# The second pair of layers of a four-layer network: from whole stages over 256 tokens to two blocks of 128 tokens, an MLP of one beside a mixer of the other

## The chip, the cores and the metric

The kernel is one program on 1 core of one Trainium2 chip, all in fp32. The metric is device time in microseconds (us). A core has five engines that run their own instruction streams in order and meet by semaphores: PE (TensorE, matrix products), ACT (ScalarE), DVE (VectorE), POOL (GpSimd) and SP (SyncE, which here only issues transfers). PEld is TensorE's loading of weights, which can overlap a matmul.

## The reference

Two networks of two layers follow each other. The first (a chunk MLP, a gated linear attention and two mixtures of experts) isn't touched. The second takes x of 256 tokens by 1024 and does:

```python
h = mixer_sb_ssm(x, ...)                     # mixer one
x = layer_norm(ALPHA * x + h)
x = layer_norm(ALPHA * x + square(relu(x @ w1[0])) @ w2[0])     # MLP one, 1024 -> 4096 -> 1024
h = mixer_dsa(x, ...)                        # mixer two
x = layer_norm(ALPHA * x + h)
x = layer_norm(ALPHA * x + square(relu(x @ w1[1])) @ w2[1])     # MLP two

def mixer_sb_ssm(x, w_in, ..., w_out):
    q, k, v, u = split(x @ w_in, 4)          # 512 wide each
    a = stick_breaking_attention(q, k, v)    # 8 heads; keys strictly before the query
    y = gelu(s5_ssm(u))                      # complex linear recurrence along the tokens, 16 x 128 states
    y = y * sigmoid(y @ w_glu + b_glu)
    return concat(a, y) @ w_out

def stick_breaking_attention(q, k, v):       # per head
    z = q @ k.T * scale
    log_1mb = where(s < t, log_sigmoid(-z), 0)
    log_w = log_sigmoid(z) + (sum of log_1mb over the later s)
    return where(s < t, exp(log_w), 0) @ v

def mixer_dsa(x, w_in, w_out):               # keys up to and with the query
    q, k, v, qi, ki, wi = split(x @ w_in)
    score = sum over 8 index heads of relu(qi @ ki.T) * wi
    keep the 64 keys of highest score; 16 heads of softmax attention with a slope on distance
    return o @ w_out
```

A token needs only tokens before it, so everything of tokens 0 to 127 can be done before anything of tokens 128 to 255. The state of the recurrence and the keys and values are all that the second block takes from the first.

## The kernel before

`write` replays one schedule for each engine; a method of the schedule is a no-op on engines that have no part in it. Generators yield at the end of a beat, and `run` and `together` advance several works by one beat in turn, so a beat sets the order in which an engine's instructions stand. There is no planner: this order is the order of each queue. Buffers are rings (`Slots`): a user waits until the last user of its slot is done. `W` is the ring of weights, five slots of 1 MB, filled by SP's queue.

The second pair of layers is `sb_ssm`, `mlp(0)`, `dsa`, `mlp(1)`, called one after another, each over all 256 tokens. Each begins with `barrier`, at which every engine, SP too, waits for all others; so the first weights of a stage are asked for behind it. Then the 16 transposes of x (`flip`, L993).

In `sb_ssm` the u columns (L1006), the coefficients and 16 `drive` steps come first; then `state_space` and `attention` run by beats. The recurrence is cut into 16 chunks of 16 tokens: 15 local steps (DVE operations of 256 elements, 8 to a step, L2026), 15 carries of 16 elements, 15 spread steps of 240 elements. The attention does two groups of four heads: scores (L1183), logarithms (ACT), `sb_beta` (POOL's `affine_select`, L2251, sets what lies above the diagonal to zero), running sums by a triangular matrix on PE (L1192 to L1194) added on DVE (L2087), exponent (ACT, L1569), `sb_weights` (the same select), and the products with v (L1203). The select takes 128 x 2048 numbers. Then the state's read-out (L1245), the gate, the output product (L1216 and L1231, each holds half of its 1024 rows) and the norm (L1686 to L1700).

In `mlp` the up half (L1006) has 256 matmuls with 256 moving columns, each 128 x 128 weights; ACT takes the relu (L1597), DVE the square (L2127). The down half (L1260) has 128 matmuls with 512 moving columns, then the add (L2136) and the norm.

In `dsa` the index columns (L1296, L1304), eight index heads (L1316, tiles of 32 rows) beside the q, k and v columns (L1006), the choice of 64 keys on DVE (L2172), and then 16 heads: products (L1325), four transposes (L1335), products with v (L1346), with DVE at L2182 to L2198; then the output product (L1231) and the norm.

## Time and profile before

| | |
|---|---|
| median of 3 runs | 3744.42 us (3741.61 to 3750.64) |
| the profiled execution | 3742.3 us, its span 3741.1 us |
| granted TensorE clock, mean | 0.836 |
| PE, PEld busy | 2684.1 us (72%), 1155.0 us (31%) |
| DVE, ACT, POOL busy | 2001.4 us (53%), 709.8 (19%), 1495.8 (40%) |
| moved by DMA | 1043.47 MB, mean 279 GB/s, up to 409 GB/s in one of 40 slices |
| second pair of layers | from 2827.2 us to the end |

The shares are over the whole span, three quarters of which are the first network; for a question about the second they have to be read from stretches. The chain of waits goes back from the last instruction to what released it, so each piece in it was on the path; idle time elsewhere costs nothing. Two instructions of PE stand for each fp32 matmul in the counts (x504 are 252 matmuls).

### The profile page before, as it was taken

Reading aid. Unit: us, or ns where it says so; the run is one execution under the profiler, and the core shown is the slowest. Engines: PE = TensorE matmul, PEld = TensorE weight load, DVE = VectorE, ACT = ScalarE, POOL = GpSimd, SP = SyncE. Lnnn points to the kernel's source line nnn. Section 1 sums busy time; section 2 is a strip of 40 time slices with the busy share of each in tenths; the row PEclk is TensorE's granted clock in tenths of the full one; section 3 lists DMA queues with packets and bytes.
Section 4 is the critical chain, followed back from the end, with each engine's and each line's share of the span. In section 5 each row is a group of like instructions: output and inputs, shape, how many; then the busy total and the mean of one; then the engine's idle time right before and its main releaser. Section 6 shows DMA issues by size and latency. Waiting matters only on the chain. (4 is left out here: it accounts for less than half of the span.)

```text
span 3741.1 us, 31922 instructions
## 1 busy us (share of the span) xinstructions
PE 2684.1 (72%) x11240; PEld 1155.0 (31%) x11240; DVE 2001.4 (53%) x4678; ACT 709.8 (19%) x1726; POOL 1495.8 (40%) x1563
## 2 busy tenths in 40 slices
PE   7758787787556776665687575565658369988898
PEld 2213332221112321111343221111116238555673
DVE  1155576654767677876214577777655941017201
ACT  0012222311113322211221121121113211004100
POOL 0034465554776676677200267767760010000000
PEclk9869988799877897767798687777678689999999
DMA  8577898999999999999432599999993104431343
GB/s 289 195 266 281 336 353 331 343 390 397 409 409 348 382 409 370 353 409 409 187 135 79 192 357 409 409 374 398 409 409 132 45 34 169 164 123 68 108 162 113
DMA packets 330484, 1043.47 MB, mean 279 GB/s; under 512 B 31748, under 2 KB 33028, under 8 KB 329812
## 3 DMA queue, kind: packets, MB, share of 16 engines
q0 software_dynamic: 221184, 805.40, 55.6%
q1 hardware_dynamic: 108724, 235.79, 17.5%
q8 instruction: 90, 1.47, 0.2%
q14 instruction: 70, 0.57, 0.0%
q10 hardware_dynamic: 416, 0.23, 0.0%
HBM read 1040.16 MB, written 1.15 MB: 278 GB/s over the span
## 5 line engine op out<-in xcount | busy, mean ns | idle before, releaser
L1072 PE MATMUL PS<-BIG,dg 64*64 64x512 f32 x6144 | 1012.6, 790 | 656.9 <-DMA BIG<-in_p_v_dram,IDX 433.6
L2225 POOL DMA_INDIRECT BIG<-in_p_u_dram,IDX x768 | 737.1, 960 | 988.4 <-ACT PS L1441 466.4
L1840 DVE CUSTOM_DVE_ANT_0 BIG<-BIG,PS 128x1024 f32<-128x1024 f32 x768 | 930.0, 1215 | 319.9 <-DMA BIG<-in_p_u_dram,IDX 315.5
L2225 POOL DMA_INDIRECT BIG<-in_p_v_dram,IDX x768 | 731.3, 952 | 310.3 <-issue 140.2
L1072 PEld LDWEIGHTS PS<-BIG,dg 64*64 64x64 f32 x6144 | 264.5, 165 | 1325.2 <-issue 853.3
L1006 PE MATMUL PS<-HT,WR 128*128 128x256 f32 (+1 forms) x1632 | 367.7, 387 | 11.9 <-DMA WR<-in_mlp_w_dram 5.3
L1006 PEld LDWEIGHTS PS<-HT,WR 128*128 128x128 f32 (+1 forms) x1632 | 310.8, 192 | 70.3 <-issue 22.8
L1006 PE MATMUL PS<-WR,HT 128*128 128x512 f32 x672 | 319.0, 628 | 11.3 <-DMA WR<-in_b_w_in_dram 6.0
L1454 ACT ACTIVATE dg<-twin,ACTV 128x64 f32<-128x64 f32 x768 | 207.9, 336 | 331.2 <-PE PS L1072 221.2
L1260 PE MATMUL PS<-WR,BIG 128*128 128x512 f32 x512 | 220.3, 592 | 1.9 <-DVE BIG L2127 1.9
L971 PE MATMUL PS<-WR,scS 128*2 128x512 f32 x384 | 178.7, 618 | 39.5 <-DMA WR<-in_w_mod_dram 39.1
L1006 PEld LDWEIGHTS PS<-WR,HT 128*128 128x128 f32 x672 | 131.1, 201 | 191.0 <-issue 184.2
L1260 PEld LDWEIGHTS PS<-WR,BIG 128*128 128x128 f32 x512 | 97.1, 190 | 124.2 <-issue 121.5
L2127 DVE TENSOR_TENSOR BIG<-BIG 128x256 f32<-128x256 f32 x64 | 27.2, 425 | 201.6 <-ACT BIG L1597 201.6
L2268 POOL IOTA BIG<- 128x512 f32 x1 | 0.6, 567 | 299.0 <-DVE X L1700 299.0
L2136 DVE SCALAR_TENSOR_TENSOR X<-X,PS 128x512 f32<-128x512 f32 x8 | 5.5, 686 | 204.7 <-PE PS L1260 204.7
L1433 ACT ACTIVATE WT<-WT 128x16 f32<-128x16 f32 x48 | 10.3, 216 | 490.1 <-DVE WT L1826 490.0
L1662 DVE TENSOR_TENSOR mrow<-mrow,PS 2x512 f32<-2x512 f32 x24 | 16.2, 676 | 147.5 <-PE PS L971 147.5
L993 PE MATMUL PS<-ident,H 128*128 128x128 f32 x152 | 31.8, 374 | 86.5 <-DVE H L1710 43.5
L2251 POOL TENSOR_SCALAR_AFFINE_SELECT BIG<-BIG 128x2048 f32<-128x2048 f32 x4 | 19.9, 4964 | 178.2 <-DVE BIG L2081 144.1
L1034 PE MATMUL PS<-WR,HT 128*128 128x512 f32 x192 | 89.3, 619 | 2.5 <-issue 1.7
L1762 DVE MAX8 V<-SCU 128x8 f32<-128x128 f32 x192 | 56.6, 295 | 60.4 <-ACT SCU L1425 50.9
(271 smaller groups left out, 2456.6 us busy)
## 6 DMA issues: line engine op xcount, KB each, us to landing
WR<-in_mlp_w_dram SPq DMA_DIRECT2D x64, 1024.0 KB, 5.6
WR<-in_w_mod_dram SPq DMA_DIRECT2D x48, 1024.0 KB, 11.1
WR<-in_b_w_in_dram SPq DMA_DIRECT2D x18, 1024.0 KB, 9.5
WR<-in_a_w_in_dram SPq DMA_DIRECT2D x16, 1024.0 KB, 10.7
WR<-in_p_w_q_dram SPq DMA_DIRECT2D x16, 1024.0 KB, 8.3
BIG<-in_p_u_dram,IDX POOLq DMA_INDIRECT x768, 9.3
BIG<-in_p_v_dram,IDX POOLq DMA_INDIRECT x768, 9.3
WR<-in_a_w_out_dram SPq DMA_DIRECT2D x8, 1024.0 KB, 10.3
```

The source lines that it names most:

```text
L971: mm = self.e.matmul(ps[0:2, :], m.scS[:, k, :], w[:, k % 4, :], start=k == 0, stop=k == 7)
L993: mm = self.e.transpose(ps[:, j * 128:(j + 1) * 128], src[:, k * 128:(k + 1) * 128], m.ident[:, :])
L1006: mm = self.e.matmul(ps[0:p, 0:n], lhs, rhs, start=k == 0, stop=k == kts - 1)
L1034: mm = self.e.matmul(ps, self.HT_of(k, b), m.slab_of(slab, k // 4)[:, k % 4, :], start=k == 0, stop=k == 7)
L1072: mm = self.e.matmul(pv[64 * i:64 * i + 64, 2 * r + n, :], dg[p, :], row[p, n * 512:n * 512 + 512], start=h == 0 and j == 0, stop=h == 7 a ...
L1260: return self.e.matmul(m.PO.of("mlp", l, b)[:, n, :], m.F[:, k + kk, b * 128:(b + 1) * 128], w[:, kk, n * 512:(n + 1) * 512], start=k + kk ...
L1454: self.e.activation(dg[:, :], m.twin[:, :], ACT.Copy, scale=m.ACTV[:, u % 4, i:i + 1]).then_inc(*self.done("diagonal", l, u, i))
L1762: e.max(top, sc).then_inc(*self.done())
L1840: self.e.tensor_tensor_reduce(row, row, xp, 1.0, 0.0, ALU.mult, ALU.add, m.ACTV[:, u % 4, j:j + 1]).then_inc(*self.done("dot", l, u, j))
L2127: self.e.tensor_tensor(m.F[:, f, :], rl, rl, ALU.mult).then_inc(*self.done("squared", l, f))
L2225: self.e.indirect_dma_start(row, None, m.A[f"p_{table}"], bass.IndirectOffsetOnAxis(ap=m.IDX[:, u % 4, j:j + 1], axis=0)).then_inc(*m.GR.l ...
L2251: self.e.affine_select(out=x, in_=x, compare_op=ALU.is_gt, fill=0.0, base=0, pattern=[[0, 4], [-128, 2], [1, 256]], channel_multiplier=-1) ...
```

## The change

The four calls become `tail`. It runs mixer one for block 0 (tokens 0 to 127) alone, and then four steps with two works advanced beat by beat: MLP one of block 0 beside mixer one of block 1; MLP one of block 1 beside mixer two of block 0; MLP two of block 0 beside mixer two of block 1; and MLP two of block 1 alone. Between the steps `barrier` stays for PE, ACT, DVE and POOL, but SP only notes it and goes on.

An MLP now works on one block: 256 up matmuls with 128 moving columns, 64 down matmuls with 512, squares of 512 elements, and PSUM rings of its own (`UP`, `DOWN`). Its weights come through `W` by SP's queue as before, but once for each block: 33.5 MB for a block and layer. Mixer weights come through a new ring `WB` of four slots of 1 MB, asked for by POOL's queue (`side_half`, `side_one`), also once for each block. Block 0 computes its 128 keys only. The recurrence has 8 chunks of 16 tokens to a block: steps of 128 and 112 elements; block 1 takes the state at the end of block 0 (`s_end`). The select works on 128 x 512 numbers, the diagonal part alone. In `drive` ACT writes the scaled part to its place and DVE adds to it. The output is stored in two halves.

```diff
-        self.sb_ssm()
-        self.mlp(0)
-        self.dsa()
-        self.mlp(1)
+        self.tail()
...
-    def sb_ssm(self):
-        m, w = self.m, self.m.A["sb_ssm_w_in_2"][0]
-        self.barrier("sb")
...
+    def tail(self):
+        self.barrier("tail")
+        self.tail_begin()
+        self.sb_early(0)
+        run(self.sb(0))
+        for step, (early, *works) in enumerate((
+                (lambda: self.sb_early(1), self.mlp(0, 0), self.sb(1)),
+                (lambda: self.dsa_early(0), self.mlp(0, 1), self.dsa(0)),
+                (lambda: self.dsa_early(1), self.mlp(1, 0), self.dsa(1)),
+                (lambda: None, self.mlp(1, 1)))):
+            early()
+            self.barrier("tail", step)
+            run(*works)
+    def sb_early(self, b):
+        m = self.m
+        self.side_slab(("sb_in", b, 3), m.A["sb_ssm_w_in_2"][0], 1536)
+        self.side_one(("br", b), m.A["s5_br"])
+        self.side_one(("bi", b), m.A["s5_bi"])
+    def sb(self, b):
+        m, w = self.m, self.m.A["sb_ssm_w_in_2"][0]
+        q, k, v, u = (("sb_in", b, n) for n in range(4))
+        self.flip(("sb", b), b, m.X[:, b, :])
+        after = self.flipped(("sb", b), [b])
+        yield
+        self.columns(u, 4, self.block_of(b), m.s_u, after)
+        if b == 0:
+            self.coefficients()
+        self.side_slab(q, w, 0)
+        yield
+        for j in range(16):
+            self.drive(b, j)
+            if j % 2:
+                yield
+        self.side_slab(k, w, 512)
+        yield from together(self.state_space(b), self.attention(b, q, k, v))
+        for c in range(4):
+            self.ssm_read(b, c)
+        yield
+        for c in range(4):
+            self.glu(b, c)
+        yield
+        self.sb_gate(b)
+        yield
+        yield from self.out_and_norm(("sb_out", b), b, (m.A["ln_mix_g_2"][0], m.A["ln_mix_b_2"][0]), m.both,
+                                     [m.act.at("sbo", b, 7), m.dve.at("sb gated", b)])
+    def state_space(self, b):
+        if b == 0:
+            for n in range(16):
+                self.power(n)
+                if n % 2:
+                    yield
+        for n in range(1 - b, 16):
+            self.local_scan(b, n)
+            yield
+        for c in range(1, 8):
+            self.carry_scan(b, c)
+            if c % 2:
+                yield
+        for n in range(15):
+            self.spread_scan(b, n)
+            yield
+    def attention(self, b, q, k, v):
+        m, w = self.m, self.m.A["sb_ssm_w_in_2"][0]
+        self.columns(q, 4, self.block_of(b), m.a_q, ())
+        self.side_slab(v, w, 1024)
+        yield
+        self.columns(k, 4, self.block_of(b), m.a_k[:, :, b * 128:(b + 1) * 128], ())
+        self.side_one(("cr", b), m.A["s5_cr"])
+        self.side_one(("ci", b), m.A["s5_ci"])
+        yield
+        self.rows_of(v, self.block_of(b), m.a_v[:, :, b, :])
+        self.side_slab(("glu", b), m.A["ssm_w_glu_2"][0], 0, kts=4)
+        yield
+        for g in range(2):
+            for i in range(4):
+                self.sb_scores(b, g, i)
+                if i % 2:
+                    yield
+            self.sb_logs(b, g)
+            yield from beats(2)
+            self.sb_beta(b, g)
+            yield from beats(2)
+            for i in range(4):
+                self.sb_sums(b, g, i)
+                if i % 2:
+                    yield
+            self.sb_weights(b, g)
+            yield from beats(2)
+            for i in range(4):
+                self.sb_outs(b, g, i)
+                if i % 2:
+                    yield
+    def mlp(self, l, b):
+        m, tag = self.m, ("mlp", l, b)
+        self.flip(tag, 2, m.X[:, b, :])
+        after = self.flipped(tag, [2])
+        for n in range(8):
+            self.load_slab(("w1", l, b, n), m.A["mlp_w1_2"][l], n * 512)
+            for j in range(4):
+                self.up(l, b, n, j, after)
+                if n and j == 1:
+                    self.square(l, b, n - 1)
+                yield
+        self.square(l, b, 7)
+        gain, shift = (*tag, "g"), (*tag, "b")
+        self.load_bc(gain, m.A["ln_ffn_g_2"][l], ())
+        self.load_bc(shift, m.A["ln_ffn_b_2"][l], ())
+        self.down_begin(l, b)
+        for k in range(0, 32, 2):
+            self.load_w2(l, b, k)
+            self.down(l, b, k)
+            yield
+        self.mlp_out(l, b)
+        self.norm_block(tag, b, gain, shift)
+    def dsa(self, b):
+        m = self.m
+        self.flip(("dsa", b), b, m.X[:, b, :])
+        self.dsa_begin(b)
+        yield
+        self.dsa_index(b)
+        yield
+        yield from together(self.select(b), self.dsa_project(b))
+        self.dsa_products(b, 0)
+        for h in range(16 + 3):
+            if h + 1 < 16:
+                self.dsa_products(b, h + 1)
+            if h < 16:
+                self.dsa_scores(b, h)
+            if 2 <= h < 18:
+                self.dsa_spread(b, h - 2)
+            if 3 <= h:
+                self.dsa_outs(b, h - 3)
+            yield
+        yield from self.out_and_norm(("dsa_out", b), b, (m.A["ln_mix_g_2"][1], m.A["ln_mix_b_2"][1]),
+                                     lambda k: m.d_out[:, k, :], [m.act.at("dsa out", b, 15)])
...
+    def up(self, l, b, n, j, after):
+        m, slab = self.m, ("w1", l, b, n)
+        ps = m.UP.of(l, b, n) if j else m.UP.take(l, b, n)
+        self.wait_ge(*after, *m.UP.emptied(l, b, n))
+        for k in range(8):
+            self.wait_ge(m.W.landed(slab, k // 4))
+            mm = self.e.matmul(ps[:, j * 128:(j + 1) * 128], m.slab_of(slab, k // 4)[:, k % 4, j * 128:(j + 1) * 128],
+                               m.HT[:, k, 256:384], start=k == 0, stop=k == 7)
+        mm.then_inc(*self.done("up", l, b, n, j))
+        if j == 3:
+            for k in range(2):
+                m.W.free((slab, k), self.done.last())
+    def down(self, l, b, k):
+        m = self.m
+        ps, w = m.DOWN.of(l, b), cut(m.W.of("w2", l, b, k), 2)
+        self.wait_ge(m.dve.at("square", l, b, k // 4), m.W.landed("w2", l, b, k))
+        for kk in range(2):
+            for n in range(2):
+                mm = self.e.matmul(ps[:, n, :], m.F[:, k + kk, :], w[:, kk, n * 512:(n + 1) * 512], start=k + kk == 0,
+                                   stop=k + kk == 31)
+        mm.then_inc(*self.done("down", l, b, k))
+        m.W.free(("w2", l, b, k), self.done.last())
...
+    def square(self, l, b, n):
+        m = self.m
+        rl = m.RM.of(l, b, n).rearrange("p (f t) -> p f t", f=4)
+        self.wait_ge(m.act.at("relu", l, b, n))
+        self.e.tensor_tensor(m.F[:, 4 * n:4 * n + 4, :], rl, rl, ALU.mult).then_inc(*self.done("square", l, b, n))
+        m.RM.free((l, b, n), self.done.last())
...
+    def side_half(self, slab, w, k, n0, n):
+        m = self.m
+        view = m.WB.take(slab, k // 4)
+        self.wait_ge(*m.WB.emptied(slab, k // 4))
+        self.e.dma_start(cut(view, 4, cols=n), w.rearrange("(k p) n -> p k n", p=128)[:, k:k + 4, n0:n0 + n]).then_inc(
+            *m.WB.landing(slab, k // 4))
+    def causal(self, x, *name):
+        self.e.affine_select(out=x, in_=x, compare_op=ALU.is_gt, fill=0.0, base=0,
+                             pattern=[[0, 4], [1, 128]], channel_multiplier=-1).then_inc(*self.done(*name))
+    def sb_weights(self, b, g):
+        m = self.m
+        self.wait_ge(m.act.at("sb weights", b, g))
+        self.causal(m.ll[:, :, b, :], "sb weights", b, g)
...
+    def barrier(self, *name):
+        if name[0] == "tail":
+            self.done.note("barrier", *name)
+        else:
+            super().barrier(*name)
```

PE, the sums and products with v of the second group of heads in mixer one. Before (L1192 to L1194 the sums, L1203 the products with v, L1216 the output product):

```order
L1192 MATMUL PS<-BIG,SC 128x256
L1193 MATMUL PS<-BIG,ones 128x256
L1194 MATMUL PS<-BIG,SC 128x256
L1192 MATMUL PS<-BIG,SC 128x256
L1193 MATMUL PS<-BIG,ones 128x256
L1194 MATMUL PS<-BIG,SC 128x256
L1203 MATMUL PS<-BIG,H 64x256 x8
L1216 MATMUL PS<-WR,X 128x512 x16
L1245 MATMUL PS<-BIG,WR 128x256 x32
```

After, in the step with MLP one of block 0 (L1226 to L1229 the sums, L1238 the products with v, L1301 the down half of the MLP):

```order
L1301 MATMUL PS<-WR,BIG 128x512 x4
L1226 MATMUL PS<-H,SC 128x128
L1228 MATMUL PS<-H,ones 128x128
L1229 MATMUL PS<-H,SC 128x128
L1226 MATMUL PS<-H,SC 128x128
L1228 MATMUL PS<-H,ones 128x128
L1229 MATMUL PS<-H,SC 128x128
L1301 MATMUL PS<-WR,BIG 128x512 x12
L1238 MATMUL PS<-H,HT 64x128 x4
L1301 MATMUL PS<-WR,BIG 128x512 x4
L1238 MATMUL PS<-H,HT 64x128 x4
L1301 MATMUL PS<-WR,BIG 128x512 x40
```

Down matmuls of the MLP now stand between the sums and the products with v. Twelve of them, three beats, stand where PE had nothing.

POOL, the whole of the second pair of layers before (L2251 the select):

```order
L2247 AFFINE_SELECT SC<-ones 128x128
L2251 AFFINE_SELECT BIG<-BIG 128x2048 x4
L2268 IOTA BIG 128x512
L2275 AFFINE_SELECT BIG<-BIG 128x512
L2282 AFFINE_SELECT BIG<-BIG 128x512
```

After, its beginning (L2290 the select, L2280 and L2287 transfers into the ring `WB`):

```order
L2272 AFFINE_SELECT SC<-ones 128x128
L2280 DMA BIG<-in_sb_ssm_w_in_dram 128x4x512 x2
L2287 DMA BIG<-in_s_br_dram 128x2048
L2287 DMA BIG<-in_s_bi_dram 128x2048
L2280 DMA BIG<-in_sb_ssm_w_in_dram 128x4x512 x6
L2287 DMA BIG<-in_s_cr_dram 128x2048
L2287 DMA BIG<-in_s_ci_dram 128x2048
L2280 DMA BIG<-in_ssm_w_glu_dram 128x4x512
L2290 AFFINE_SELECT H<-H 128x4x128 x4
L2280 DMA BIG<-in_sb_ssm_w_out_dram 128x4x512 x4
L2280 DMA BIG<-in_sb_ssm_w_in_dram 128x4x512 x2
```

POOL had seven instructions and no transfers there. Now a block's transfers stand around the selects in one queue, and those of the output product are behind them.

PE, the heads of mixer two. Before (L1325 products, L1335 transposes, L1346 products with v):

```order
L1325 MATMUL PS<-BIG 128x256 x2
L1335 MATMUL PS<-ident,BIG 128x128 x4
L1346 MATMUL PS<-BIG 64x256 x2
L1325 MATMUL PS<-BIG 128x256 x2
L1335 MATMUL PS<-ident,BIG 128x128 x4
L1346 MATMUL PS<-BIG 64x256 x2
L1325 MATMUL PS<-BIG 128x256 x2
```

After (L1342, L1350 and L1360 the same in that order, L1283 the up half of MLP one of block 1):

```order
L1350 MATMUL PS<-ident,X 128x128 x2
L1283 MATMUL PS<-HT,WR 128x128 x8
L1342 MATMUL PS<-H 128x256
L1350 MATMUL PS<-ident,X 128x128 x2
L1360 MATMUL PS<-X,H 64x128 x2
L1283 MATMUL PS<-HT,WR 128x128 x8
L1342 MATMUL PS<-H 128x256
L1350 MATMUL PS<-ident,X 128x128 x2
L1360 MATMUL PS<-X,H 64x128 x2
```

Each head has half of the matmuls, and eight up matmuls stand between two heads.

## Rows read from the trace of the kernel before

**Rows 1.** The chain of waits, 2990 to 3742 us: start, length (us), what, times.

```profile
3089.99 8.08 DMA WR<-in_mlp_w_dram
3098.11 109.06 PE PS L1006 x504
3208.09 110.15 PE PS L1260 x256
3318.27 0.70 DVE X L2136
...
3324.73 5.13 DMA WR<-in_dsa_w_dram
...
3467.09 27.75 PE PS L1231 x64
...
3501.39 5.85 DMA WR<-in_mlp_w_dram
3507.37 112.19 PE PS L1006 x512
3620.48 110.15 PE PS L1260 x256
```

**Rows 2.** Windows, both mixers: PE, PEld, DVE, ACT, POOL busy (instructions), clock, DMA share, GB/s.

```profile
2876.00:3090.00 214.00, 114.95 (x425) 77.72 (x424) 165.56 (x495) 40.93 (x52) 19.86 (x4) 0.79 0.15 54
3391.00:3467.00 76.00, 61.21 (x272) 40.26 (x270) 63.23 (x148) 36.23 (x103) 1.24 (x2) 0.93 0.16 56
```

**Rows 3.** Timeline of PE, PEld, 125 to 127 us: start, length, 128 moving columns.

```profile
125.72 1.86 PEld L1020 LDWEIGHTS PS<-BIG,WR 128*128 128x128 f32 x16 [0.86 <-issue]
125.73 2.05 PE L1020 MATMUL PS<-BIG,WR 128*128 128x128 f32 x16
```

**Rows 4.** Timeline of PE, 3371 to 3380 us, index heads between columns.

```profile
3371.78 3.72 PE L1006 MATMUL PS<-HT,WR 128*128 128x256 f32 x16
3375.44 1.13 PE L1316 MATMUL PS<-BIG 32*128 32x256 f32 x4
3376.49 3.72 PE L1006 MATMUL PS<-HT,WR 128*128 128x256 f32 x16
```

**Rows 5.** Timeline of PE, the beginning of mixer one.

```profile
2827.40 3.65 PE L993 MATMUL PS<-ident,X 128*128 128x128 f32 x16 [2.04 <-DVE X L1700]
2834.95 15.48 PE L1006 MATMUL PS<-HT,WR 128*128 128x256 f32 x64 [3.90 <-DMA WR<-in_sb_ssm_w_in_dram]
...
2861.28 12.63 PE L1170 MATMUL PS<-H,WR 128*128 128x256 f32 x48 [6.66 <-DVE BIG L2019]
```

**Rows 6.** Timeline, all engines, 3007 to 3027 us, around a select.

```profile
3012.23 13.54 POOL L2251 TENSOR_SCALAR_AFFINE_SELECT BIG<-BIG 128x2048 f32<-128x2048 f32 x1 [21.08 <-ACT BIG L1569]
...
3013.62 1.92 DVE L2026 TENSOR_TENSOR SC<-BIG,SC 128x240 f32<-128x240 f32 x4
...
3017.04 1.95 DVE L2026 TENSOR_TENSOR SC<-BIG,SC 128x240 f32<-128x240 f32 x4
...
3022.95 1.06 DVE L2026 TENSOR_TENSOR BIG<-BIG,SC 128x240 f32<-128x240 f32 x2
...
3025.83 1.55 PE L1203 MATMUL PS<-BIG,H 128*64 128x256 f32 x6 [27.39 <-POOL BIG L2251]
```

**Rows 7.** Timeline, all engines, 2955 to 2962 us, around the same select of the group before.

```profile
2957.01 2.07 DVE L2026 TENSOR_TENSOR s5c<-s5c 128x16 f32<-128x16 f32 x2
2957.11 1.95 POOL L2251 TENSOR_SCALAR_AFFINE_SELECT BIG<-BIG 128x2048 f32<-128x2048 f32 x1 [13.03 <-ACT BIG L1569]
...
2959.22 0.48 DVE L2026 TENSOR_TENSOR s5c<-BIG,SC 128x16 f32<-128x16 f32 x4
...
2960.05 0.48 DVE L2026 TENSOR_TENSOR s5c<-BIG,SC 128x16 f32<-128x16 f32 x4
```

**Rows 8.** Page of the profile, DMA issues: KB each, us from issue to landing.

```profile
WR<-in_mlp_w_dram SPq DMA_DIRECT2D x64, 1024.0 KB, 5.6
...
BIG<-in_p_u_dram,IDX POOLq DMA_INDIRECT x768, 9.3
```

More of the change, by code:

```diff
@@ new lines, in side_of, with rows_of @@
+    def side_of(self, slab, k, n=512):
+        return cut(self.m.WB.of(slab, k // 4), 4, cols=n)[:, k % 4, :]
+    def rows_of(self, slab, lhs, dst):
+        m = self.m
+        ps = m.PS.take("rows", slab)
+        self.wait_ge(*m.PS.emptied("rows", slab))
+        for k in range(8):
+            self.wait_ge(m.WB.landed(slab, k // 4))
+            mm = self.e.matmul(ps, lhs(k), self.side_of(slab, k), start=k == 0, stop=k == 7)
+        mm.then_inc(*self.done("rows", slab))
+        for k in range(2):
+            m.WB.free((slab, k), self.done.last())
```

964 lines of the change are left out of this document (409 added, 555 removed).

## The prediction

> **What bounds the kernel now.** The chain of waits of the second pair of layers comes first. It should be read for who carries each stretch and for what stands between two stretches [rows 1]. From 2827.2 us (the strict mask) to the end at 3741.1 there are four stages: mixer one to 3089.6, MLP one to 3324.7, mixer two to 3501.3, MLP two to the end; together 913.9 us. In the MLPs the chain is TensorE and nothing else: 109.1 us of up matmuls and 110.2 us of down matmuls, then again 112.2 and 110.2. Between them stand a norm (3318.27 to 3324.73, 6.5 us after the last matmul) and a load that starts only behind the barrier (8.1, 5.1 and 5.9 us). The windows say what the mixers lose [rows 2]: in 2876 to 3090 TensorE is busy for 115 of 214 us and VectorE for 165.6, and in the heads of mixer two TensorE is busy for 61 of 76 us. So there are about 99 + 15 us in mixers in which TensorE stands, 19 us of loads behind barriers, and four norms. That is what running an MLP beside a mixer can take back.
>
> **What the change costs on TensorE.** An fp32 matmul shows as two instructions. Before, an up matmul moves 256 columns: 109.06 us for 504 instructions is 0.2164 us each [rows 1]. Now it moves 128. Its price is seen at the one place where 128 columns move with 128x128 weights: 16 weight loads take 1.86 us [rows 3], so with the last load of 0.19 us taken off it is 0.111 us from one to the next, where half of 0.2133 would be 0.107. The weight load then is the longer part of the pair. One block's up half costs 512 x 0.1114 = 57.0 us, twice that is 114.0 instead of 109.1. Down still moves 512 columns and is split evenly: 55.1 us per block. One block's MLP is 112.1 us; the change adds about 5 us of TensorE per layer.
>
> Mixer work of block 1 on TensorE beside MLP one, at 0.111 or 0.430 us an instruction: columns of u, q, k 21.4, v 6.8, drive 7.1, scores 3.6, sums 5.3, outs 3.4, state read 7.1, GLU 3.6, output 13.7; 72 us. Mixer two is 56.7 us for block 0 (half of the keys) and 67.3 for block 1. Interleaving shapes is not free: between two groups of 16 matmul instructions with four of 32 rows between them the period is 3376.49 - 3371.78 = 4.71 us [rows 4], where 20 instructions at 0.2133 would be 4.27: 0.44 us for a change there and back. Mixer two now has about 34 such pairs in a step (8 index heads, and 16 heads of one to two changes each), which is 15 us; mixer one about 7, which is 3 us. The bounds are 0 (a change hides under the next weight load) and 30.
>
> **What a step costs beside its streams.** Between steps all four computing engines still meet. From the last matmul to the barrier is the add and the norm, 7.1 us with the evacuation (6.5 from [rows 1]); behind it the flip's eight transposes (sixteen took 3.65 us at a low clock, [rows 5]) and their evacuation, 4.6. Per step 11.7. The loads behind barriers go, since SyncE no longer waits and has five slots filled.
>
> **Step by step.**
> The first block of mixer one runs alone. Its u slab lands 10 us after the start (before: 2834.95 us, 7.6 after 2827.4, [rows 5]), columns to 20, coefficients to 29.5, half of the 12.6 us of drives [rows 5] to 38, the powers of the coefficients (some 10) to 48; then VectorE waits for the first logs until 64, as TensorE must first do q, k and v, whose loads now come from GpSimd's queue. Then scans. A step of eight operations takes 3017.04 - 3013.62 = 3.42 us at 240 elements [rows 6] and 0.83 us at 16 (2959.22 to 2960.05) [rows 7]; at 128 the line between them gives 2.1, at 112 2.0. 15 local steps, 7 carries and 15 spreads: 67 us. Between them the attention's VectorE work 10. Behind them state read 7.6, GLU and gate 6.6, output 13.7, norm 7.1. Sum 176.
> Step 0, MLP one of block 0 beside mixer one of block 1: 112.1 + the mixer's flip 2.1 + 72 + 3 + 1 for the slow first beat + 11.7 = 202.
> Step 1, beside mixer two of block 0: 112.1 + 2.1 + 56.7 + 15 + 4 (k slab late once) + 11.7 = 202.
> Step 2: 202 + 10.6 for the longer keys = 212.
> Step 3, MLP two of block 1 alone: 112.1 + 2.1 + 11 = 125. End, the store of the output: 4.
> Together 921 us against 913.9. All that is taken back in the mixers is spent: block 0's mixer alone costs 176 instead of 262 / 2 (the fixed parts and the load wait are paid again), the doubled instruction counts at 128 columns cost 10, changed tile shapes 33, and one more barrier, flip and norm than before. VectorE has 67 + 53 us of work in the 202 us of step 0, so it doesn't bound it by its sum.
>
> **The masks are where this sum breaks.** GpSimd's select behind the weights took 13.54 us at 3012.23 us and the one before it in the same place 1.95 us [rows 6, 7]. Size and code are the same. In the long case VectorE ran scan operations with two inputs in SBUF back to back until it had none left (to 3024.0), and the select ended 1.7 us after; TensorE had waited 27.4 us. In the short case the operations had 16 elements. So GpSimd gets SBUF when VectorE pauses; with short operations at once, with operations of 240 elements not at all. The Trainium skill ("SBUF — State Buffer", Who interferes with whom) has the same pair of engines lock each other out, but for one instruction each; by it a select would wait one operation, about half a microsecond, and the sum would stay at 921. The row with 13.5 us across some 28 operations disagrees, and the measurement decides.
> Now VectorE's steps have 128 and 112 elements, between both rows. The order gives the place: in step 0 the weights of group 0 are released before beat 22 and TensorE has three up beats of 1.8 us (5.3 us) until it needs them, while VectorE has about five local steps in hand, 10.7 us; group 1 has three down beats of 3.4 us (10.3) against twelve spread steps, 23.5 us. If the select gets nothing, TensorE waits 7 (with its own 2 us) + 15 = 22 us. In block 0's mixer, where VectorE is the bound anyhow, it costs some 2 us. That is 945 us, so a span of 2827.2 + 945 = 3772 and, 1.2 us around it as in the profiled run (3742.3 against 3741.1), 3773.5. The profiled execution lies 2.1 us under the median of the runs, so 3775 as a median. The bounds of this term are 0 (as at 16 elements) and 37 (no cover at all, 10.7 + 23.5 + the select). I take 24, since 112 and 128 elements are operations of about 0.35 us that follow each other as those of 240 do.
>
> **The loads of GpSimd.** No row shows a plain load of 1 MB from GpSimd's queue. The nearest are SyncE's, 5.6 us to landing, and GpSimd's indirect ones of 0.5 MB, 9.3 us [rows 8]. I take 8. The Trainium skill ("DMA: Bandwidth & Descriptors", Bandwidth) has 1 MB from GpSimd at 6.15 us; the sum would lose 2 us in block 0's mixer by it. A step moves 33.5 MB for the MLP and 13 to 17 for the mixer in 200 us, 250 GB/s, where slices of the page reach 409.
>
> **Rivals.**
> A, the forecast: locked-out selects, 3775. Chance 0.42.
> B, the selects get through: 921 us, 3748 + 1.2 + 2.1 = 3752. For it: the short case [rows 7]. 0.26.
> C, faster: selects get through and changes of tile shape hide under weight loads, 921 - 33 = 888, so 3718. For it: half of the weight loads are 0.19 us beside matmuls of 0.43, with room. Against: the row of 4.71 us. 0.24.
> D, slower by far: mixer slabs late. GpSimd's queue runs in order, so a select stuck for 10 to 20 us holds the output's slabs behind it, and a slab asks for a slot that the last user has yet to free. At each of three steps 15 to 25 us, 3775 + 60 = 3835; it decides when a load behind a select lands later than TensorE reaches it. 0.08.
>
> **The numbers.** Forecast 3775. B and C on one side and part of D on the other give 3713 to 3800. A measurement of this kernel tells 0.3%, 11 us, from no change. Faster: C 0.22, a low B 0.04. Same: B 0.15, C 0.02, A 0.03. Slower: A 0.39, B 0.07, D 0.08.
>
> **What would show it.** The first barrier near 3003 us, the others near 3227, 3429 and 3641. In step 0 two selects of over 5 us with TensorE idle before the outs; if they take about 0.7 us, A is wrong. Up matmuls at 0.111 us an instruction, and groups of 20 that take 0.44 us more than their sum. If TensorE is busy for over 95% of steps 1 and 2 at less than 195 us, the 15 us of shape changes are wrong and C is near. If TensorE's idle time ends with DMAs into the new ring, it is D.

## The result, and the profile after

| | before | after |
|---|---|---|
| median (7 runs each) | 3744.42 us (3735.78 to 3755.01) | 3766.48 us (3755.99 to 3775.33) |
| ratio of the times, 95% interval | | 1.0056 [1.0035, 1.0077] |
| profiled execution, span | 3742.3, 3741.1 us | 3755.99, 3754.7 us |
| second pair of layers | 913.9 us | 934.7 us |
| TensorE busy, idle in it | 754.2, 159.7 us | 787.7, 147.0 us |

The kernel is slower by 0.56%. The first network, which isn't touched, happened to take 7 us less in the profiled execution after, which was the fastest of the seven, 10.5 us under their median. So the stages are compared and not the spans. Runs of one kernel spread by 19 us. A stage of the profile spreads less, as long as GpSimd's selects in it take the same time, so the stages are the better measure where a few us matter.

The windows of the kernel after, one for each of its five stages. Columns as in [rows 2].

```profile
2820.00:2994.20 174.20, 81.57 (x456) 65.73 (x456) 103.71 (x479) 37.55 (x85) 28.73 (x26) 0.70 0.44 162
2994.20:3210.00 215.80, 195.96 (x1168) 148.23 (x1169) 107.16 (x387) 43.62 (x88) 15.05 (x21) 0.94 0.68 243
3210.00:3414.80 204.80, 191.63 (x1057) 139.95 (x1057) 46.59 (x144) 29.79 (x93) 11.30 (x17) 0.95 0.67 239
3414.80:3627.30 212.50, 201.75 (x1105) 144.53 (x1105) 57.42 (x144) 34.04 (x93) 8.43 (x13) 0.96 0.61 218
3627.30:3754.70 127.40, 116.77 (x648) 85.43 (x648) 12.69 (x19) 5.58 (x10) 0.00 (x0) 0.94 0.67 239
```

And those of the four stages before:

```profile
2827.20:3089.60 262.40, 152.12 (x577) 108.94 (x577) 184.63 (x552) 60.48 (x97) 20.15 (x5) 0.80 0.20 72
3089.60:3324.70 235.10, 224.77 (x784) 148.89 (x784) 28.07 (x54) 13.86 (x36) 0.00 (x0) 0.99 0.42 148
3324.70:3501.40 176.70, 151.41 (x609) 102.84 (x610) 85.29 (x187) 49.40 (x134) 1.81 (x3) 0.93 0.23 81
3501.40:3741.10 239.70, 225.90 (x784) 149.99 (x784) 28.08 (x54) 13.86 (x36) 0.00 (x0) 0.97 0.42 149
```

The reader is to see two things. The idle time of TensorE fell by 13 us only: of the 110 us in mixer one before, 93 are still there, in block 0's mixer, which has nothing beside it. And its busy time rose by 33.5 us. A busy time is longer where the granted clock is lower, so it has to be taken apart: if the pair of layers is cut into windows of 1 us, TensorE's busy time in each is multiplied by the granted clock there, and all are added up, it has 728.3 us of work at full clock before and 746.5 after (an estimate from the traces). So 18 of the 33.5 us are more work and 15 are a lower clock. Beside each other an MLP and a mixer fill TensorE to 91, 94 and 95%, so the steps do what they say. The forecast had 176, 202, 202, 212 and 129 us (without the select) and the profile has 174, 216, 205, 212.5 and 127: only step 0 is off.

The chain of waits of the kernel after, where [rows 1] had the MLPs in one piece each (start, length, what, times):

```profile
2895.98 11.74 POOL H L2290
...
2973.57 14.02 PE PS L1272 x32
...
2994.26 1.94 PE PS L999 x8
...
3187.13 16.20 PE PS L1272 x32
...
3210.01 1.94 PE PS L999 x8
...
3386.93 20.61 PE PS L1301 x48
...
3414.79 1.94 PE PS L999 x8
...
3599.43 20.61 PE PS L1301 x48
...
3627.28 1.94 PE PS L999 x8
...
3630.05 59.91 PE PS L1283 x512
3689.96 54.95 PE PS L1301 x128
```

The up half of the last MLP, which stands alone, takes 59.9 us for 512 instructions: twice that is 120 where [rows 1] has 109 for both blocks. (Its first 5 us had a granted clock of 0.50.) The output product at 3187.13 takes 16.2 us, at 2973.57 14.0: TensorE had stood for 6.3 us and the clock had fallen, with 0.86 granted in those 16.2 us and 1.00 in the 14.0. From 3386.93 + 20.61 us to 3414.79, and from 3599.43 + 20.61 to 3627.28, stand the two boundaries, 7.2 us each.

The same place on the timeline (engine, line, operation, idle time before it and what ended it), the end of step 0:

```profile
3177.11 3.73 PE L1260 MATMUL PS<-BIG 128*128 128x128 f32 x32
...
3183.91 2.56 DVE L1733 TENSOR_TENSOR X<-X,BC 128x1024 f32<-128x1024 f32 x2
3186.38 0.69 DVE L2149 TENSOR_TENSOR BIG<-BIG 128x512 f32<-128x512 f32 x1
...
3187.13 16.19 PE L1272 MATMUL PS<-BIG 128*128 128x512 f32 x32 [6.28 <-DVE BIG L2149]
```

VectorE's two long operations of the MLP's norm (L1733) stand ahead of the gate (L2149), and TensorE waits 6.3 us for the gate. Nothing in the forecast's sum had that.

The selects, which were the forecast's 24 us. In block 0's mixer and in step 0, on the timeline:

```profile
2895.98 11.73 POOL L2290 TENSOR_SCALAR_AFFINE_SELECT H<-H 128x512 f32<-128x512 f32 x1 [7.29 <-ACT H L1601]
...
3085.63 0.74 POOL L2290 TENSOR_SCALAR_AFFINE_SELECT H<-H 128x512 f32<-128x512 f32 x1 [9.16 <-ACT H L1601]
...
3118.66 0.72 POOL L2290 TENSOR_SCALAR_AFFINE_SELECT H<-H 128x512 f32<-128x512 f32 x1 [9.71 <-ACT H L1601]
```

In step 0 they took 0.7 us each. That in block 0's mixer took 11.7 us. It stands in the chain of waits, since TensorE's products and, behind them, the logs of the second group of heads wait for it, but it only just hid: VectorE took up these logs at 2914.11 us without an idle time before it and went on without a pause until 2957.

### The profile page after: what moved, and what is told of

Its sections match the earlier page's. It is cut to its first block, busy times and chain, and to the rows that moved or that the text cites. A ratio compares the mean times of both kernels' runs of the same rounds, so it can differ in the third digit from the quotient of the medians.

```text
span 3754.7 us, 35721 instructions
## 1 busy us (share of the span) xinstructions
PE 2697.8 (72%) x12920; PEld 1223.2 (33%) x12920; DVE 2004.3 (53%) x5005; ACT 722.9 (19%) x1792; POOL 1540.9 (41%) x1632
## 3 DMA queue, kind: packets, MB, share of 16 engines
q0 software_dynamic: 236256, 867.34, 59.9%
## 4 chain that ended last, share of the span: by engine, by line
PE 45%; DMA 24%; DVE 17%; ACT 5%; POOL 5%; issue 3%; SPq 0%; DVEq 0%; ACTq 0%; POOLq 0%
DMA BIG<-in_p_u_dram,IDX 11%; PE PS L1012 9%; PE PS L1078 8%; DMA BIG<-in_p_v_dram,IDX 7%; DVE BIG L1873 6%; PE PS L1301 6%; PE PS L1283 5%; POOL BIG L2250 4%; DMA WR<-in_w_mod_dram 3%; PE PS L977 3%; PE PS L1040 2%; PE PS L1178 2%; PE PS L1272 2%; PE PS L988 1%; ACT dg L1468 1%
## 5 line engine op out<-in xcount | busy, mean ns | idle before, releaser
L1012 PE MATMUL PS<-WR,HT 128*128 128x512 f32 x640 | 300.9, 623 | 11.4 <-DMA WR<-in_b_w_in_dram 6.1
L1283 PE MATMUL PS<-HT,WR 128*128 128x128 f32 x2048 | 258.3, 287 | 8.4 <-DMA WR<-in_mlp_w_dram 5.0
L1283 PEld LDWEIGHTS PS<-HT,WR 128*128 128x128 f32 x2048 | 248.1, 201 | 18.0 <-issue 6.2
L1301 PE MATMUL PS<-WR,BIG 128*128 128x512 f32 x512 | 227.3, 598 | 0.0
L977 PE MATMUL PS<-WR,scS 128*2 128x512 f32 x384 | 179.1, 620 | 38.9 <-DMA WR<-in_w_mod_dram 38.6
L1301 PEld LDWEIGHTS PS<-WR,BIG 128*128 128x128 f32 x512 | 95.8, 191 | 115.0 <-issue 115.0
L2168 DVE TENSOR_TENSOR BIG<-BIG 128x512 f32<-128x512 f32 x32 | 22.1, 691 | 161.0 <-ACT BIG L1630 160.8
L1178 PE MATMUL PS<-HT,BIG 128*128 128x128 f32 x768 | 93.0, 283 | 8.4 <-DMA BIG<-in_sb_ssm_w_in_dram 6.9
L1695 DVE TENSOR_TENSOR mrow<-mrow,PS 2x512 f32<-2x512 f32 x24 | 16.2, 676 | 147.4 <-PE PS L977 147.4
L1178 PEld LDWEIGHTS PS<-HT,BIG 128*128 128x128 f32 x768 | 90.7, 199 | 10.5 <-issue 5.5
L977 PEld LDWEIGHTS PS<-WR,scS 128*2 128x2 f32 x384 | 31.4, 87 | 182.7 <-issue 145.2
L1040 PE MATMUL PS<-WR,HT 128*128 128x512 f32 x192 | 88.9, 618 | 2.5 <-issue 1.7
L2280 POOL DMA_DIRECT2D BIG<-in_dsa_w_dram x20 | 14.9, 752 | 183.2 <-PE PS L1272 109.9
```

The costliest lines, as they stand in the source:

```text
L977: mm = self.e.matmul(ps[0:2, :], m.scS[:, k, :], w[:, k % 4, :], start=k == 0, stop=k == 7)
L1012: mm = self.e.matmul(ps[0:p, 0:n], lhs, rhs, start=k == 0, stop=k == kts - 1)
L1040: mm = self.e.matmul(ps, self.HT_of(k, b), m.slab_of(slab, k // 4)[:, k % 4, :], start=k == 0, stop=k == 7)
L1178: mm = self.e.matmul(ps[:, i * 128:(i + 1) * 128], self.side_of(slab, k)[:, i * 128:(i + 1) * 128], rhs(k), start=k == 0, stop=k == 7)
L1283: mm = self.e.matmul(ps[:, j * 128:(j + 1) * 128], m.slab_of(slab, k // 4)[:, k % 4, j * 128:(j + 1) * 128], m.HT[:, k, 256:384], start=k ...
L1301: mm = self.e.matmul(ps[:, n, :], m.F[:, k + kk, :], w[:, kk, n * 512:(n + 1) * 512], start=k + kk == 0, stop=k + kk == 31)
```

## The experiments

Times of stages are from one profiled execution each; where a ratio stands it is to the kernel before on the same chip, with its 95% interval. The last four runs were on a slower chip (before: 3926 us), so their ratios count and not their times.

**One after another.** The works of the changed kernel, none beside another:

```diff
-                (lambda: self.sb_early(1), self.mlp(0, 0), self.sb(1)),
-                (lambda: self.dsa_early(0), self.mlp(0, 1), self.dsa(0)),
-                (lambda: self.dsa_early(1), self.mlp(1, 0), self.dsa(1)),
-                (lambda: None, self.mlp(1, 1)))):
+                (lambda: self.sb_early(1), self.sb(1)), (none, self.mlp(0, 0)), (none, self.mlp(0, 1)),
+                (lambda: self.dsa_early(0), self.dsa(0)), (lambda: self.dsa_early(1), self.dsa(1)),
+                (none, self.mlp(1, 0)), (none, self.mlp(1, 1)))):
```

> All works of the changed kernel, by blocks and with their own rings, but none beside another: mixer one of block 0, mixer one of block 1, MLP one of both blocks, mixer two of both, MLP two of both, each behind a barrier. Theory Q (the step beside each other works, and what is lost is that block 0's mixer runs alone and that work by blocks costs more TensorE time): four MLPs of 125 us each as in the last step now, mixer one of block 1 about 160, mixer two 95 and 105, so the second pair of layers takes about 174 + 160 + 500 + 95 + 105 + 3 = 1037 us where the changed kernel takes 935; TensorE is busy there for about 755 us where it is 788 now, as changes of tile shape between MLP and mixer (33 us in the forecast) are gone. Rival R (changes of shape cost nothing, the added TensorE time is the 128 columns and low clocks): TensorE busy for 780 us or more.

Its windows: mixer one of block 1, an MLP, mixer two of block 0, and the whole.

```profile
3005.40:3157.40 152.00, 87.80 (x520) 72.90 (x520) 93.78 (x368) 37.72 (x78) 21.25 (x17) 0.76 0.26 92
3281.70:3406.90 125.20, 117.07 (x649) 85.77 (x650) 12.70 (x19) 5.58 (x10) 3.00 (x5) 0.95 0.76 266
3406.90:3509.90 103.00, 83.98 (x409) 60.50 (x409) 34.16 (x125) 23.66 (x83) 11.24 (x17) 0.73 0.53 188
2833.50:3878.40 1044.90, 813.34 (x4432) 604.84 (x4432) 327.28 (x1173) 149.56 (x369) 62.37 (x77) 0.84 0.56 197
```

The whole took 1044.9 us where 1037 were expected, and 110 more than beside each other. So working by blocks, with a barrier around each work, costs 131 us against the whole stages before (913.9), and the steps win 110 of them back. The second part of the expectation fell: TensorE is busy for 813 us, more than the 788 beside each other. That lies in rival R's range (780 or more), but it doesn't show R, because the clock in the mixers alone was 0.76 and 0.73 (0.94 and 0.95 in the steps), and a busy time at another clock can't be subtracted. Multiplied by the granted clock in each microsecond, as above, it is 728.5 us of work at full clock, against 728.3 in the kernel before and 746.5 beside each other. So the blocks alone cost TensorE no more work: the 131 us are 72 of idle time and 59 of a lower clock. And running two works beside each other costs 18 us, 8.5 in step 1, 9.3 in step 2 and nothing in step 0, where the forecast had 33 for the changes of tile shape (15, 15 and 3). A row of the kernel after shows one such change:

```profile
3263.13 0.48 PE L1334 MATMUL PS<-H 32*128 32x128 f32 x2
...
3263.54 2.05 PE L1283 MATMUL PS<-HT,WR 128*128 128x128 f32 x16
...
3265.52 0.48 PE L1334 MATMUL PS<-H 32*128 32x128 f32 x2
```

18 instructions in 3265.52 - 3263.13 = 2.39 us, where 18 at 0.1114 would be 2.01: 0.38 us for a change there and back, 0.44 in the forecast.

**64 columns.** In the last step the up matmuls move 64 columns; the kernel leaves out the other 64 tokens there:

```diff
+        c = 64 if (l, b) == (1, 1) else 128
...
-            mm = self.e.matmul(ps[:, j * 128:(j + 1) * 128], m.slab_of(slab, k // 4)[:, k % 4, j * 128:(j + 1) * 128],
-                               m.HT[:, k, 256:384], start=k == 0, stop=k == 7)
+            mm = self.e.matmul(ps[:, j * 128:j * 128 + c], m.slab_of(slab, k // 4)[:, k % 4, j * 128:(j + 1) * 128],
+                               m.HT[:, k, 256:256 + c], start=k == 0, stop=k == 7)
```

> The changed kernel, with the up matmuls of the last step (MLP two of block 1, alone) moving 64 columns instead of 128; half of the tokens are left out there. Theory Q (with 128 columns the weight load sets the pace, at 0.111 us an instruction): the 512 instructions of the up half take 57 to 60 us as now (59.9). Rival (columns set the pace, half of 0.2133 = 0.107 at 128): 29 to 35 us.

```profile
3638.60:3748.10 109.50, 109.47 (x513) 109.50 (x514) 4.84 (x7) 4.18 (x7) 0.00 (x0) 0.50 0.42 144
```

And the same stretch of the kernel after, with 128 columns:

```profile
3630.00:3690.00 60.00, 59.95 (x513) 59.97 (x514) 4.85 (x7) 4.18 (x8) 0.00 (x0) 0.96 0.73 258
```

It was neither number but 109.5 us. PEld was busy throughout, and the granted clock was 0.50, where it was 0.96 with 128 columns. At the lower level (1.2 GHz) 109.5 us for half the columns are as many cycles as 54.7 us at the upper one, 0.107 us an instruction. The rival's 29 to 35 us would be 58 to 70 at this clock, so it is out: halving the columns saved next to no cycles, and with 64 columns the weight load sets the pace, as Theory Q had it. With 128 columns the weight load (0.107) and half of 0.2133 are the same to within a row's precision, and both lie just below the 0.111 measured; which of them sets the pace there isn't shown. That the clock stayed at the lower level nobody had forecast.

**A wait for the select, one beat later.** VectorE waits for GpSimd's select behind the weights:

```diff
             self.sb_weights(b, g)
-            yield from beats(2)
+            yield
+            self.sb_pause(b, g)
+            yield
...
+    def sb_pause(self, b, g):
+        self.wait_ge(self.m.pool.at("sb weights", b, g))
```

> The changed kernel, with VectorE waiting for GpSimd's select behind the weights one beat after it is released, so that the select can't be shut out for longer than a scan step. Theory P (the forecast: shut-out selects cost TensorE 22 us in step 0 and 2 in block 0's mixer): step 0 falls from 216 to about 194, the first stage by 2. Theory Q (in step 0 the selects took 0.7 us anyway, and in block 0's mixer VectorE has no idle time between 2886 and 2957 us, so that the 11.7 us select hides): the first stage 174 within 2, step 0 216 within 3; the long select is gone from the trace.

The first stage took 172.1 us and step 0 214.4, 2 and 1.4 less than after, as Theory Q had it: there were no 22 us in step 0 to be won. The select in the first stage took 3.8 us. But the other runs, none of which touched it, show that it isn't the same from one execution to the next:

| first stage | select behind the weights, group 0 | the stage |
|---|---|---|
| one after another | 1.5 us | 171.9 us |
| 64 columns | 3.8 | 174.2 |
| after | 11.7 | 174.2 |
| MLP a beat later | 18.2 | 179.1 |
| without two barriers | 18.2 | 180.7 |
| after, again | 18.2 | 181.1 |

VectorE has scan steps for 18 us in hand there. In the run with the MLP a beat later, on the timeline:

```profile
2902.58 18.20 POOL L2295 TENSOR_SCALAR_AFFINE_SELECT H<-H 128x512 f32<-128x512 f32 x1 [7.30 <-ACT H L1606]
...
2920.83 1.12 PE L1243 MATMUL PS<-H,HT 128*64 128x128 f32 x8 [23.42 <-POOL H L2295]
...
2927.17 0.69 DVE L2126 SCALAR_TENSOR_TENSOR H<-H 128x512 f32<-128x512 f32 x1 [6.83 <-ACT H L1600]
```

VectorE ran out of scan steps at 2920.3, the select ended half a us later, and VectorE then waited 6.8 us for the logs of the second group. From the start of this select to that of the next one, behind those logs, it is 19.6 us where the select took 1.5, 3.8 and 11.7 us, and 26.1 where it took 18.2. So a select of up to 11.7 us is hidden and one of 18.2 costs 6.5 us, in the stage for which the forecast had 2. (The 2.3 us between the first two rows of the table lie outside of this stretch.)

**The MLP a beat later** in step 0 (`late(self.mlp(0, 0), 1)`).

> The changed kernel, with MLP one of block 0 starting one beat after mixer one of block 1 in step 0. Theory Q (of the 14 us by which step 0 is longer than forecast, 6.3 are TensorE waiting for the gate, which on VectorE stands behind the MLP's add and norm): the gate now stands ahead of the norm and two down matmuls cover it, so the wait of 6.3 us before the output product goes and step 0 falls from 216 to about 209. Rival V (the step is bound by its TensorE stream and the wait moves elsewhere, to the norm of the MLP at the end): 214 or more.

Step 0 took 201.3 us, 14.5 less, where Theory Q had 7. The output product followed without a wait and at full clock:

```profile
3183.63 3.60 PE L1306 MATMUL PS<-WR,BIG 128*128 128x512 f32 x8
3187.07 13.90 PE L1277 MATMUL PS<-BIG 128*128 128x512 f32 x32
```

The wait gave 6.3 us and the clock in the output product 2.3. TensorE's waits for the selects ahead of the sums (L1226 in the kernel after) fell from 5.9 to 2.1, and the other 2 us are a higher clock in the rest of the step (0.97 over the step, 0.94 before this edit). Together that is all by which step 0 had missed the forecast of 202 us. The median of this edit alone wasn't taken.

**Without two barriers.** The MLP's next transposes ahead of its norm, mixer two of block 1 four beats later:

```diff
+        run(self.mlp(0, 1, then=(1, 0)), self.dsa(0))
+        self.dsa_early(1)
+        run(self.mlp(1, 0, True, then=(1, 1)), late(self.dsa(1), 4))
+        run(self.mlp(1, 1, True))
...
         self.mlp_out(l, b)
+        if then:
+            self.flip(("mlp", *then), 2, m.X[:, then[1], :], m.dve.at("normed block", ("dsa_out", then[1])))
         self.norm_block(tag, b, gain, shift)
```

> The changed kernel, without the barriers ahead of steps 2 and 3: the transposes for the next MLP stand before the norm of the MLP that ends, mixer two of block 1 starts four beats later, and only data are waited for. Theory Q (each of the two boundaries costs 7.3 us from the last matmul to the barrier, 2.8 of transposes and their evacuation, and some 4 of slow clock behind it): 20 to 28 us less, the second pair of layers about 911 instead of 935 us and the ratio to before 0.998 to 1.000. Rival W (what is taken away comes back as waits of mixer two or late weights): less than 10 us, ratio 1.003 or more.

The three last stages took 523.2 us instead of 544.7: 21.5 less, as Theory Q had it, 13.4 of it idle time and 8.1 a lower clock. The ratio was 1.0013 [1.0001, 1.0025], 16 us less than 1.0056 and a little above Theory Q's 1.000; its profiled first stage was one with an 18.2 us select. The boundary on TensorE, where before this edit it was idle for 7.3 us and had a slow first beat:

```profile
3403.74 20.76 PE L1310 MATMUL PS<-WR,BIG 128*128 128x512 f32 x48
3424.34 1.04 PE L1008 MATMUL PS<-ident,X 128*128 128x128 f32 x8
3426.53 9.17 PE L1292 MATMUL PS<-HT,WR 128*128 128x128 f32 x80 [1.15 <-ACT HT L1405]
```

**q, k and v of block 0 through the MLP's ring**, and the q columns ahead of the drives.

```diff
+        if not b:
+            for n in (0, 1, 2):
+                self.load_slab(("sb_in", 0, n), m.A["sb_ssm_w_in_2"][0], n * 512)
...
         if b == 0:
             self.coefficients()
+            self.columns(q, 4, self.block_of(b), m.a_q, ())
```

> The changed kernel, with the q, k and v weights of block 0's mixer one loaded into the MLP's ring by SyncE, which is idle then, and the q columns ahead of the drives. Theory Q (block 0's mixer alone is 174 us because VectorE waits to 2886 us, 66 us from its start, for the first logs, and TensorE stood 8.1 us for the coefficients while q wasn't there): logs and everything behind them 7 us earlier, the first stage about 166 us. Rival X (the columns only change places and the drives come later): 172 or more.

The first stage took 168.8 us, between both theories. The q columns now run inside the wait for the coefficients:

```profile
2845.41 6.52 PE L1188 MATMUL PS<-HT,WR 128*128 128x128 f32 x56 [0.72 <-DMA WR<-in_sb_ssm_w_in_dram]
...
2854.60 6.41 PE L1214 MATMUL PS<-BR,BIG 128*128 128x128 f32 x48 [0.88 <-DVE BIG L2063]
```

but the select took 17.9 us here. In the next run, with the same edit and a select of 1.5 us, the stage is 161.7 us, ten less than the 171.9 with such a select and the old order. (168.8 against 161.7 us is the price of the long select once more.) In the execution of 168.8 us a select was held up in step 0 too: it took 8.2 us, TensorE waited 4.8 us for it ahead of the products with v, and step 0 took 221.4 us, 5.6 more than after. So what the forecast feared in step 0 does happen, in one of the seven profiles of this step without a wait.

**All three edits.**

> The three edits together: MLP one of block 0 a beat later, no barriers ahead of steps 2 and 3, q, k and v of block 0 through the other ring. Theory Q: 6 + 24 + 7 = 37 us less than the changed kernel, the second pair of layers about 898 us against 914 in the kernel before, so a ratio to before of 0.995 to 0.997. Theory P (the forecast's sum, in which the shut-out selects made the loss): at most 15 us less, ratio 1.001 or more.

The ratio was 0.9916 [0.9902, 0.9930], the median 3712.58 us against 3742.12: faster than both kernels, and by more than expected, since step 0 and the first stage gave 26 us and not 13. Its windows: block 0's mixer, step 0, the rest.

```profile
2825.30:2987.10 161.80, 77.45 (x457) 61.99 (x457) 103.10 (x479) 37.17 (x85) 13.91 (x20) 0.72 0.47 174
2987.10:3189.00 201.90, 191.60 (x1169) 146.15 (x1169) 106.78 (x387) 43.34 (x88) 19.71 (x22) 0.96 0.72 259
3189.00:3711.30 522.30, 501.86 (x2808) 361.91 (x2808) 116.47 (x307) 69.24 (x196) 19.64 (x30) 0.97 0.68 241
```

Together they take 886.0 us, 48.7 less than the kernel after, of which 12.5 in the first stage, 13.9 in step 0 and 22.4 in the rest. Taken apart as above, the second pair of layers is, in us:

| | before | one after another | after | all three edits |
|---|---|---|---|---|
| TensorE's work at full clock (estimate) | 728.3 | 728.5 | 746.5 | 746.5 |
| added by a lower clock | 25.9 | 84.8 | 41.2 | 24.4 |
| idle | 159.7 | 231.6 | 147.0 | 115.1 |
| together | 913.9 | 1044.9 | 934.7 | 886.0 |

The edits took nothing off TensorE's work. All that they won was idle time and the lower clock that goes with it.

**The select's price in the median.** The kernel after again; the same with VectorE's wait in the beat of the release (`self.sb_pause(b, g)` right behind `self.sb_weights(b, g)`); and all three edits with this wait.

> The changed kernel itself, as the measure for the next ones on the same chip. In the profiles so far the select behind the weights in block 0's mixer took 1.5, 3.8, 3.8, 11.7, 18.2, 18.2 and 17.9 us, with the first stage at 172 to 174 us where it took under 12 and at 179 to 181 where it took 18. Both theories: ratio to before 1.0035 to 1.008.

> The changed kernel, with VectorE waiting for the select behind the weights in the beat in which it is released, so that it is shut out for one scan step at most. Theory P' (the shut-out select costs the usual execution 7 us in the first stage and now and then 6 in step 0, and the profiled execution, the fastest of seven, was a lucky one): the median falls by 6 to 12 us against the changed kernel in the same call, ratio to before near 1.003. Theory Q (the select hides in both stages): at most 3 us, ratio unchanged.

> The three edits (MLP one of block 0 a beat later, no barriers ahead of steps 2 and 3, q, k and v of block 0 through the other ring) and the wait of VectorE for the select. Theory Q: as without the wait, 0.9916, within 0.001. Theory P' (executions in which the select is shut out are rid of 7 us): 0.990 to 0.991, and a smaller spread.

The kernel after again has 1.0060 [1.0041, 1.0079]. With the wait it is 1.0036 [1.0019, 1.0053], 6.7 us less in the median of 3947, as Theory P' had it. The select of the kernel after again and that of the kernel with the wait, and who waited for it:

```profile
3085.42 18.23 POOL L2290 TENSOR_SCALAR_AFFINE_SELECT H<-H 128x512 f32<-128x512 f32 x1 [7.32 <-ACT H L1601]
```

```profile
3080.75 1.79 POOL L2295 TENSOR_SCALAR_AFFINE_SELECT H<-H 128x512 f32<-128x512 f32 x1 [7.30 <-ACT H L1603]
...
3082.57 0.37 DVE L2061 TENSOR_TENSOR SC<-X,s5c 128x128 f32<-128x128 f32 x1 [0.48 <-POOL H L2295]
...
3082.59 1.12 PE L1240 MATMUL PS<-H,HT 128*64 128x128 f32 x8 [7.01 <-POOL H L2295]
```

VectorE gives up 0.5 us and TensorE gets its products 16 us earlier; the stage is 174.2 us instead of 181.1. The intervals of the two ratios overlap, so the size rests on the stage. With all three edits it was 0.9939 [0.9917, 0.9961], outside of what either theory expected, and its interval overlaps that of 0.9916. The second pair of layers took 885.8 us in it and 886.0 without the wait, whose select happened to take 1.5 us: so the wait was worth nothing in these two profiles, and whether it is worth something in the median stays open.

**The same wait in the kernel before**, a beat behind the release, and in the beat of the release.

> The kernel before, with VectorE waiting for GpSimd's select behind the weights one beat (one scan step) after it is released. Theory S (the select of the second group, 13.5 us long, holds up the products with v and the first half of the output product, 14.0 us, which then stand before the read-out of the state): the select takes about 2 us, the products with v start at about 3014.5 instead of 3025.8 us, and the read-out 11 to 12 us earlier; mixer one 262 to about 251 us, the ratio to before about 0.997. Rival T (the scans end at 3024 us and a wait of VectorE moves them to 3026, and TensorE waits for these): at most 2 us gained, ratio 1.000.

> The kernel before with the same wait in the same place, one scan step earlier than in the run with the wait a beat later (select 6.7 us, mixer one 257.5 us, ratio 0.9978). Theory S: the select ends at about the end of the first scan step behind its release plus 2 us, some 4 us earlier, and the mixer takes 253 us; ratio 0.9965 to 0.998. Rival T (the scans end later by the wait and hold TensorE): ratio 0.998 or more.

The first gave 0.9978 [0.9969, 0.9987], the second 0.9982 [0.9966, 0.9998]. The select and the products with v in each, where [rows 6] has 13.54 us and 27.4 us of waiting:

```profile
3016.82 6.68 POOL L2257 TENSOR_SCALAR_AFFINE_SELECT BIG<-BIG 128x2048 f32<-128x2048 f32 x1 [21.07 <-ACT BIG L1572]
...
3023.56 0.30 PEld L1206 LDWEIGHTS PS<-BIG,H 128*64 128x64 f32 x4 [20.58 <-POOL BIG L2257]
```

```profile
3202.69 3.24 POOL L2256 TENSOR_SCALAR_AFFINE_SELECT BIG<-BIG 128x2048 f32<-128x2048 f32 x1 [21.06 <-ACT BIG L1571]
...
3205.98 3.53 PE L1205 MATMUL PS<-BIG,H 128*64 128x256 f32 x16 [17.09 <-POOL BIG L2256]
```

Mixer one took 257.5 and 254.3 us, 4.9 and 8.1 less than before. Theory S holds, and rival T (2 us at most) doesn't. The first run gained less than the 11 us expected because two scan steps stood before its wait and not one, so the select still took 6.7 us; the second came within 1.3 us of the 253 expected. The medians can't tell the two apart, and the second run's 0.9982 by itself lies in the range of its rival T; it is the stage, and the first run's interval, that speak against T.

## Why the prediction came out as it did

The time (3775, range 3713 to 3800) was near, and the direction was right. The mechanism on which it stood was not what made the kernel slower: by its own sign (two selects in step 0 of over 5 us; if about 0.7 us, A is wrong) A failed, with 0.7 us. By its steps:

- **Block 0's mixer alone, 176 us**: right, 174.2 as a sum. VectorE got the first logs at 2886.4 us, 66 us from the start, where the forecast had 64.
- **128 columns cost 0.111 us an instruction**: right, with 1.79 us for 16 inside the steps. The forecast's reason, that the weight load is the longer part, is shown for 64 columns and not for 128. By the estimate at full clock the four MLPs by blocks cost 452.4 us against 445.7 before, 7 more where the forecast had 10.
- **Changes of tile shape, 0.44 us**: 0.38 in one row. The sum of 33 us was too large for what stands between two works: by the estimate at full clock the steps cost 18 us more than their works one after another.
- **Steps 1 to 3**: 202, 212 and 129 forecast, 204.8, 212.5 and 127.4 measured. In steps 1 and 2 two errors made up for each other: the 15 us for shapes were 8.5 and 9.3, and mixer two by itself was 4 and 2 us dearer at full clock (62.6 and 71.7 where the forecast had 58.8 and 69.4 with the flip); the rest is a lower clock, for which the sum had almost nothing.
- **Step 0, 202 us and 22 for the selects**: this is the step that failed, in both terms. The selects took 0.7 us there in the profiled execution, so the 22 us did not come; the longest in any profile of this step took 8.2 us. The 202 were 216, because the gate stands behind the MLP's norm on VectorE (6.3 us), TensorE's clock fell in that wait (2.3), and the sums waited for logs and selects (5.9; of this 3.8 went with the beat). The forecast took the number of beats as the cover and didn't look at what the end of one work puts in front of the other on a shared engine. Moving the MLP by one beat gave all of it back (201.3 us).
- **"In block 0's mixer, where VectorE is the bound anyhow, it costs some 2 us"**: mis-sized. When the select is shut out for the whole 18 us, VectorE isn't the bound any more, since its own next work waits for what the select holds up. It costs some 6.5 us, and it happened in four of the eight profiles without a wait for it (17.9 to 18.2 us). The wait took 0.24% off the ratio of the kernel after, with intervals that overlap. In the profiled execution after (11.7 us) it cost nothing.
- So the 24 us for the selects were nothing in this profile and some 6.5 us in four of eight profiles, in the other stage, and the 14 us that step 0 missed made up for most of them. That the time came out near, and that the kernel was slower as forecast, is luck. Without the term the sum of 921 us would have forecast 3752, no change. Rival B (3752) had the same sum and missed the 14 us of step 0; rival C's gain didn't come: steps 1 and 2 took 205 and 212.5 us, though by the estimate some 15 of its 33 us were indeed not paid.
- **Late slabs (D)**: no. TensorE waited 1.5 us for a mixer's slab in step 1 and 3.1 for an MLP's; the sum had 4 for a late slab there. The two input weights of the mixers, a megabyte each time from GpSimd's queue, took 7.5 and 8.2 us to land in the median, where the forecast had 8; the other megabytes of this queue had medians from 5.6 to 12.2 us.

The Trainium skill ("SBUF — State Buffer", Who interferes with whom) has one instruction's length as the price of the shared port. Most of the selects in step 0 agree with that (0.7 to 1.7 us). Those of 8 to 18 us, across some 30 to 65 VectorE instructions, do not, and the measurement decides; what decides between the two cases isn't shown by any run.

## What to carry to other kernels

Before two works are put beside each other, count what has nothing beside it: here the first block's mixer alone kept 93 us of idle time, where the whole mixer had 110 before. Take idle time, a lower clock and work apart before a busy time is compared: here 15 of 33.5 us more busy time were the clock. At the end of a step look at each shared in-order engine for what one work puts ahead of the other one's last operation; shifting one work by a beat was worth 14 us, taking out two barriers 21.5. And where an engine can shut another out for as long as it has work, try a wait on purpose: it took the stage from 181.1 to 174.2 us here and from 262.4 to 254.3 in the kernel before, where the ratio was 0.9978; with all three edits no gain from it was measured.

## What the runs showed of the hardware

- GpSimd's select beside VectorE operations with two inputs in SBUF, back to back: the same instruction took 1.5, 3.8, 11.7 and 18.2 us in executions whose code is the same up to there. It always ended once VectorE paused, and sometimes before: while that of 11.7 us ended, at 2907.71 us, a VectorE operation took 0.78 us and its neighbours 0.41 and 0.35. In step 0 it took 0.7 to 1.7 us in most profiles, 3.8 and 8.2 in two, and 3.8 and 2.8 with the wait a beat later; in block 1's mixer alone it took 9.7.
- Matmuls that move 64 columns behind 128 x 128 weights ran at a granted clock of 0.50 for 109 us on end, with PEld busy without a gap; with 128 columns it was 0.96 over 60 us, after 0.50 in the first 5.
